# Three stages of a hybrid decoder step: samples' block scores by sample, first decay totals inside the gate projection, prompt scores from rounded halves

## The reference, cut to what matters

```python
# NSA, prompt and samples: compressed blocks, the 16 selected blocks, a window of 512
s_c = einsum('btgrd,bngd->bgrtn', q, kc) * scale - slopes * dist_c
p_c = masked_softmax(s_c, dist_c >= 0)
_, idx = top_k(score_of(p_c), 16)                      # blocks of 64 rows
ss = einsum('grd,gkld->grkl', q, k[idx]) * scale - slopes * dist    # selected
ss = einsum('bqgrd,bkgd->bgrqk', q, k_win) * scale - slopes * dist  # window
# both recurrences, in chunks, per head
b = cumsum(logf)
o = (q * exp(b)) @ S + tril(q k^T decayed by exp(b_t - b_s)) @ v
S = exp(b_last) * S + (k * exp(b_last - b))^T v
```

## Time and profile before

| | us |
|---|---|
| median of 3 runs | 4044.45 (4039.71 to 4048.02) |
| profiled execution, own time | 4041.04 |
| its span | 4039.4 |
| TensorE matmul busy | 3489.2 (86%) |
| VectorE, ScalarE, GpSimd busy | 1353.9, 1344.8, 1483.8 |

### The profile page before, as it was taken

The page is one execution under the profiler, slowest core; times in us unless marked ns, Lnnn a source line. Parts: engine busy times, 40 slices in busy tenths (PEclk is TensorE's granted clock), DMA queues, the critical chain, the costliest instruction groups (busy, mean ns, idle before and its releaser), DMA issues. The chain is left out here.

```text
span 4039.4 us, 64008 instructions
## 1 busy us (share of the span) xinstructions
PE 3489.2 (86%) x22287; PEld 3282.6 (81%) x22287; DVE 1353.9 (34%) x2028; ACT 1344.8 (33%) x2211; POOL 1483.8 (37%) x964
## 2 busy tenths in 40 slices
PE   5988887898088888799999998798997899999997
PEld 4966665898058777799999997788886799999997
DVE  3034442001003445443343332043345344343342
ACT  2134442000003443244344442233323244344442
POOL 2300001332403222246666664122222256666663
PEclk8978887899569999899999999899999899999998
DMA  1400001785200001134444443101111134444443
GB/s 71 129 17 0 0 0 48 258 266 164 78 11 32 32 32 58 59 99 139 137 138 149 144 151 106 48 28 39 51 38 54 58 114 133 138 140 133 143 137 124
DMA packets 158153, 372.99 MB, mean 92 GB/s; under 512 B 22410, under 2 KB 78026, under 8 KB 156316
## 3 DMA queue, kind: packets, MB, share of 16 engines
q1 hardware_dynamic: 116828, 310.96, 23.9%
q10 hardware_dynamic: 29440, 32.78, 2.5%
q0 software_dynamic: 11776, 27.80, 2.1%
HBM read 352.76 MB, written 22.89 MB: 93 GB/s over the span
## 5 line engine op out<-in xcount | busy, mean ns | idle before, releaser
L493 POOL TENSOR_TENSOR back_WL<-back_RAW,back_WH 128x1024 fp32r<-128x1024 f32 (+1 forms) x408 | 956.1, 2350 | 679.3 <-ACT back_WH L594 678.2
L532 PE MATMUL PS<-back_TH,back_WH 128*128 128x344 f32 x2112 | 676.9, 321 | 13.9 <-DVE back_TL L703 13.9
L532 PE MATMUL PS<-back_TL,back_WH 128*128 128x344 f32 x2112 | 674.7, 319 | 0.0
L532 PE MATMUL PS<-back_TH,back_WL 128*128 128x344 f32 x2112 | 674.4, 319 | 0.0
L594 ACT ACTIVATE back_WH<-back_RAW 128x1024 fp32r<-128x1024 f32 (+1 forms) x408 | 421.6, 1033 | 523.2 <-DMA back_RAW<-in_w 350.7
L532 PEld LDWEIGHTS PS<-back_TH,back_WH 128*128 128x128 f32 x2112 | 397.9, 188 | 15.6 <-issue 15.6
L532 PEld LDWEIGHTS PS<-back_TL,back_WH 128*128 128x128 f32 x2112 | 398.0, 188 | 0.0
L532 PEld LDWEIGHTS PS<-back_TH,back_WL 128*128 128x128 f32 x2112 | 397.8, 188 | 0.0
L741 DVE TENSOR_TENSOR back_HL<-back_TMP,back_HH 128x344 f32 x132 | 323.1, 2447 | 126.5 <-ACT back_HH L607 126.5
L1076 PE MATMUL PS<-layer_XH,layer_WH 128*128 128x344 f32 x960 | 325.9, 339 | 32.8 <-POOL layer_WL L1026 28.5
L532 PE MATMUL PS<-back_HH,back_WH 128*128 128x344 f32 x1056 | 338.4, 320 | 0.0
(11 more groups left out here) (365 smaller groups left out, 6079.3 us busy)
## 6 DMA issues: line engine op xcount, KB each, us to landing
back_RAW<-in_w SPq DMA_DIRECT2D x360, 512.0 KB, 3.3
layer_AR<-in_cmp SPq DMA_DIRECT2D x192, 128.0 KB, 4.3
layer_AR<-in_cmp POOLq DMA_DIRECT2D x192, 128.0 KB, 4.1
back_RAW<-in_w SPq DMA_DIRECT2D x48, 384.0 KB, 3.1
layer_AR<-in_cmp ACTq DMA_DIRECT2D x128, 128.0 KB, 4.1
layer_WR<-in_w_even SPq DMA_DIRECT2D x54, 256.0 KB, 2.8
layer_WR<-in_w_odd SPq DMA_DIRECT2D x50, 256.0 KB, 2.9
XT<-in_xT SPq DMA_DIRECT2D x4, 1032.0 KB, 7.8
```

Of the source, the lines that this page charges most:

```text
L493: pool.tensor_tensor(lo, raw, hi.bitcast(F32), ALU.subtract).then_inc(wl_ready, 1)
L532: mm = pe.matmul(m.PS[:, bank, 0:CH], wgt[:, t % RING, w], tok[:, k0 + k], start=(k0 + k + n == 0), stop=(last and n == 2 and k == kt - 1))
```

## The change

It does three things.

1. *Samples' block scores.* The fetch loops are written out over the samples, each sample has semaphores of its own, and TensorE takes a sample's eight instructions (two groups, two halves) as soon as its 30 blocks are in.
2. *First totals.* Chunk 0's totals move out of `steps` into the gate projection: for HGRN2 between its third and fourth piece (and the turning of the logarithms ahead of it, so TensorE waits for the logarithm first), for GLA between the two gate tiles. Chunk 1's totals follow directly behind the gate tile. `expo`, `queries` and `keys` of chunk 0 move with them; queries 1 goes behind the first product of step 0.
3. *Prompt scores.* q and the keys are split into fp32r halves. `m.QS` holds for a group q's high part on its own 64 partitions and q's low part on the others; `m.KHD` holds the high part of the keys on both halves of the partitions, `m.KL` the low part. A score is one fp32r matmul over 128 rows (high keys times both parts of q) and one over 64 rows (low keys times high q). ScalarE makes the high keys of kind 0 and VectorE their low part, GpSimd both for the window, all once ahead of the rounds; the low part of q is a VectorE subtraction per round and group.

```diff
@@ linear_attention, GpSimd @@
                 for pos in GATES:
                     lower(h, pos)
+                keys(h, 0)
                 if more:
                     lower(h + 1, 0)
-                for c in range(QT):
+                for c in range(1, QT):
                     keys(h, c)
@@ linear_attention, TensorE, opening @@
-                for pos in GATES:
-                    tile(h, pos)
                 pe.wait_ge(turn_read, h * 3 * VT + ONE)
-                if not gla:
+                if gla:
+                    tile(h, NEARLY)
+                    sums(h, 0)
+                    tile(h, NEARLY + 1)
+                else:
                     pe.wait_ge(lf_ready, h + 1 + ONE)
...
+                    for n in range(NLN):
+                        natural(h, n)
+                    for j in range(3):
+                        piece(h, NEARLY, j)
+                    pe.wait_ge(nat_read, h * NNAT + NLN + ONE)
+                    sums(h, 0)
+                    for j in range(3, 6):
+                        piece(h, NEARLY, j)
+                sums(h, 1)
+                evacuated(pe, h, ORDER.index(1 + VT))
+                for n in range(NLN, NNAT):
+                    natural(h, n)
...
             def steps(h, more):
-                sums(h, 0)
-                sums(h, 1)
                 for c in range(QT):
@@ ScalarE, opening @@
-                for pos in GATES:
-                    evac_then(h, pos, (h, pos + 1) if pos + 1 < NTL else (h + 1, 0) if more else None)
-                for n in range(NNAT):
...
+                if gla:
+                    evac_then(h, NEARLY, (h, NEARLY + 1))
+                    expo(h, 0)
+                    evac_then(h, NEARLY + 1, following)
+                else:
+                    for n in range(NLN):
+                        natural(n)
+                    evac(h, NEARLY, 0)
+                    expo(h, 0)
+                    evac(h, NEARLY, 1)
+                    if more:
+                        upper(*following)
+                    evac(h, NEARLY, 2)
+                for n in range(NLN, NNAT):
+                    natural(n)
@@ VectorE @@
+                evacuated(dve, h, ORDER.index(0))
+                queries(h, 0)
                 dve.wait_ge(smp_turned, h + 1 + ONE)
...
-                queries(0)
-                queries(1)
...
                     if c >= 1:
                         state(c - 1)
-                        if c + 1 < QT:
-                            queries(c + 1)
+                    if c + 1 < QT:
+                        queries(h, c + 1)
@@ attention, GpSimd (new) @@
+            for g in range(G):
+                for half in (halves[g], halves[1 - g]):
+                    pool.tensor_tensor(m.KHD[1][g][half], NT[halves[g], TKW, 0:SEQ],
+                                       m.ones[halves[g], 0:1].to_broadcast([DH, SEQ]), ALU.mult).then_inc(kx_ready, 1)
+            pool.wait_ge(kx_ready, 4 + ONE)
+            for half, high in zip(halves, m.KHD[1]):
+                pool.tensor_tensor(m.KL[1][half], NT[half, TKW, 0:SEQ], high[half].bitcast(F32), ALU.subtract)\
+                    .then_inc(kx_ready, 1)
@@ attention, TensorE, scores @@
-                        mm = pe.matmul(sbank(s)[:, a - k0:b - k0], m.QP[:, g, i * P:(i + 1) * P],
-                                       NT[:, TKS if kind == 0 else TKW, a:b], start=True, stop=True)
+                        pe.matmul(sbank(s)[:, a - k0:b - k0], m.QS[:, g, i * P:(i + 1) * P], m.KHD[kind][g][:, a:b],
+                                  start=True, stop=False)
+                        mm = pe.matmul(sbank(s)[:, a - k0:b - k0], m.QS[half, g, i * P:(i + 1) * P],
+                                       m.KL[kind][half, a:b], start=False, stop=True)
@@ attention, TensorE, compressed scores @@
-                        mm = pe.matmul(m.PS[:, 7, c0:c0 + PBLK], m.QP[:, g, i * P:(i + 1) * P], m.KCT,
-                                       start=True, stop=True)
+                        pe.matmul(m.PS[:, 7, c0:c0 + PBLK], m.QS[:, g, i * P:(i + 1) * P], m.KCH[:, g],
+                                  start=True, stop=False)
+                        mm = pe.matmul(m.PS[:, 7, c0:c0 + PBLK], m.QS[:, g, i * P:(i + 1) * P], m.KCL[:, g],
+                                       start=False, stop=True)
@@ attention, ScalarE @@
+            for g in range(G):
+                act.activation(m.KHD[0][g][halves[g]], NT[halves[g], TKS, 0:SEQ], ACT.Copy).then_inc(kh_ready, 1)
+            for g in range(G):
+                act.activation(m.KHD[0][g][halves[1 - g]], NT[halves[g], TKS, 0:SEQ], ACT.Copy).then_inc(kh_ready, 1)
@@ attention, VectorE @@
-            t.up(dve.memset(m.QP, 0.0))
...
+            dve.wait_ge(kh_ready, 4 + ONE)
+            for half, high in zip(halves, m.KHD[0]):
+                dve.tensor_tensor(m.KL[0][half], NT[half, TKS, 0:SEQ], high[half].bitcast(F32), ALU.subtract)\
+                   .then_inc(kl_ready, 1)
... in each round, per group, behind the bias tables:
+                    dve.wait_ge(q_ready, r * 2 + g + 1 + ONE)
+                    dve.tensor_tensor(m.QS[halves[1 - g], g:g + 1], NT[halves[g], ds(r, 1), 0:SEQ],
+                                      m.QS[halves[g], g:g + 1].bitcast(F32), ALU.subtract).then_inc(ql_ready, 1)
@@ sample_select @@
-            with eng.Fori(0, NB) as b:
+            for b in range(NB):
...
-                            .then_inc(pool_in if eng is nc.gpsimd else blocks_in, 16)
+                            .then_inc((pool_in if eng is nc.gpsimd else blocks_in)[b], 16)
...
-            pe.wait_ge(blocks_in, 20 * NB * 16)
-            pe.wait_ge(pool_in, 10 * NB * 16)
             pe.wait_ge(idx_ready, 2)
-            for half in range(2):
-                rows = slice(half * DH, (half + 1) * DH)
-                for n in range(NBG16):
+            for n in range(NBG16):
+                if n % G == 0:
+                    pe.wait_ge(blocks_in[n // G], 20 * 16)
+                    pe.wait_ge(pool_in[n // G], 10 * 16)
+                for half in range(2):
+                    rows = slice(half * DH, (half + 1) * DH)
                     mm = pe.matmul(m.PS[0:ROWS, 2 + half, :].rearrange("p (a b) -> p a b", b=BLK),
```

More of the change, by code:

```diff
@@ L1085, in tile, with natural @@
                     piece(h, pos, j)
+            def natural(h, n):
+                src = fT if n < NLN else vT[:, (n - NLN) // 2]
+                if n >= 2:
+                    pe.wait_ge(nat_read, h * NNAT + n - 1 + ONE)
+                if NLN <= n < 2 * NLN:
+                    pe.wait_ge(lnl_ready, h * NLN + n - NLN + 1 + ONE)
+                for c in range(4):
+                    j = n % 2 * 4 + c
+                    mm = turn(m.PS[:, 6 + n % 2, c * P:(c + 1) * P], src[:, j * P:(j + 1) * P])
+                mm.then_inc(nat_ready, 1)
             def opening(h):
@@ L1126, in sums @@
             def sums(h, c):
+                if c == 0:
+                    pe.wait_ge(lnl_ready, (h + 1) * (NLN or 1) + ONE)
                 pe.wait_ge(ex_ready, h * QT + c + ONE)
@@ L1291, in opening @@
                        .then_inc(nat_read, 1)
+                act.wait_ge(turn_read, h * 3 * VT + ONE)
+                following = (h + 1, 0) if more else None
+                if gla:
[13 more added lines that the diff above has]
+                    natural(n)
                 if gla:
@@ L1683, in attention, with _ @@
         ot_read = sem("ot_read")
-        zeroed = m.dve.n + 2
+        zeroed = m.dve.n + 1
+        halves = [slice(g * DH, (g + 1) * DH) for g in range(G)]
         block = ctx.enter_context(started(nc, sems))
+        @block.gpsimd
+        def _(pool):
+            for g in range(G):
[6 more added lines that the diff above has]
+                    .then_inc(kx_ready, 1)
         @block.tensor
@@ L1798, in _ @@
             t = m.dve
-            t.up(dve.memset(m.QP, 0.0))
             t.up(dve.memset(m.PC, 0.0))
+            for g in range(G):
+                for half in (halves[g], halves[1 - g]):
+                    dve.tensor_copy(m.KCH[half, g], m.KCT[halves[g]]).then_inc(kc_ready, 1)
+            dve.wait_ge(kc_ready, 4 + ONE)
+            for g in range(G):
+                for half in (halves[g], halves[1 - g]):
+                    dve.tensor_tensor(m.KCL[half, g], m.KCT[halves[g]], m.KCH[halves[g], g].bitcast(F32), ALU.subtract)\
+                       .then_inc(kc_ready, 1)
+            dve.wait_ge(kh_ready, 4 + ONE)
+            for half, high in zip(halves, m.KHD[0]):
+                dve.tensor_tensor(m.KL[0][half], NT[half, TKS, 0:SEQ], high[half].bitcast(F32), ALU.subtract)\
+                   .then_inc(kl_ready, 1)
             dve.wait_ge(t.sem, zeroed)
```

82 lines of the change are left out of this document (41 added, 41 removed).

## The result

The changed kernel takes 4228.98 us (median of 4 runs, 4222.30 to 4236.00) against 4045.13 of the kernel before in the same comparison (4 runs): a ratio of 1.0456, 95% interval 1.0432 to 1.048. It is slower by 184 us where 96 less were predicted. The profiled execution has a span of 4234.4 us, 195.0 more than before.

| stage | before | after | difference |
|---|---|---|---|
| to the first HGRN2 projection (attention and all samples' stages) | 1202.1 | 1408.9 | +206.8 |
| HGRN2, first projection to last level matmul | 422.8 | 424.5 | +1.7 |
| output projection and feed-forward of layer 0 | 879.1 | 887.6 | +8.5 |
| GLA, from there to its last level matmul | 611.3 | 583.9 | -27.4 |
| the rest, to the end of the span | 924.1 | 929.5 | +5.4 |

A forecast was written before the change was run, and what follows sets the result against it. It took TensorE's own work and the holes in it as the bound; terms -35 - 16 - 24 - 21 = -96 took 4041.0 to 3945, 3948 against the median, range 3895 to 4000.

The forecast's parts named there:

- A block costs 0.47 instead of 0.85: Prompt attention: a 512-key score block as two fp32r matmuls 0.237 us apart instead of two fp32 instructions of 0.43.
- part 3: Prompt scores from rounded fp32r halves: -21 us in all (-45 to +5), after added preparation.
- Rival A: Attention falls to half clock because shorter scores make steps too thin: +168 us, about 4150, slower; 6%.
- The heads of the rounds: Added preparation before the first compressed score: +15 us in round 0, +11.5 over rounds 1 to 3.
- the contention: Round 0: GpSimd's window-key work slows VectorE beside it, 0 to 14 us possible, 5.6 taken.
- The 10 us of the compressed scores: Compressed prompt scores: fp32r weight loads 0.11 instead of 0.22 us apart, 2.5 us saved a round, -10.
- Part 1: Samples' block scores run as each sample's blocks arrive, hiding seven of eight samples: -35 us (-28 to -44).
- The written-out loop: Samples' fetch loop unrolled: -2 us taken, between up to 8 saved and 5 lost.
- the last sample: Samples' block scores: the one burst behind the last block priced at half clock, 6.8 us; 3.4 at full clock.
- Part 2: First decay totals inside the gate projection: -16 us in the first layer, -24 in the second.
- the hole ahead of the gate tile: First layer's heads: TensorE must now wait for the logarithm before the gate tile, a new 3.6 us hole.
- 38 hoped for: Prompt attention: shorter score blocks save 9.5 us a round, -38 in all (-25 to -55).

The follow-up runs named there:

- E4: The changed kernel with 16 dense fp32r matmuls of 512 columns per round straight before the body's step 0, low keys still on 64 rows: 4019.43 us.
- E3: The changed kernel with the low-key matmul over all 128 rows instead of 64: 3966.33 us.
- E13: E3 with a matmul of 64 rows and 4 columns ahead of each block, overwritten by the block's own: 4016.57 us.
- E15: The changed kernel with both score matmuls on the group's own 64 rows, leaving out low query times high key: 4163.14 us.
- E5: The changed kernel without the low-key matmuls, one fp32r matmul over 128 rows per block of prompt scores: 3944.67 us.
- E16: E3 with the low keys of the second group set to zero, all matmuls still over 128 rows: 3972.14 us.
- E6: The changed kernel with both high, then both low matmuls in steps of two blocks, low keys on 64 rows: median 4156.13 us, ratio 1.0176.
- E1: The changed kernel without its prompt-score change (samples' block scores and first totals changed, prompt scores fp32 as before): 3968.54 us.
- E9: The kernel before with only the samples' block-score change: 3994.99 us.
- E10: E9 with TensorE waiting for all samples and matmuls in their old order, so only the fetch loops are written out: 4036.14 us.
- E8: E1 with the first two pieces of the gate tile moved ahead of the wait for the logarithm in the first layer's heads: 3950.02 us.
- E11: E9 with each sample's instructions ordered four on partitions 0 to 63, then four on 64 to 127: 4005.44 us, one run.

## Why the prediction was wrong, step by step

**The step that failed** is "A block costs 0.47 instead of 0.85" in part 3, with the clock that the sum took for granted. It counted columns and took 0.237 us from matmuls that all ran over 128 rows; the low-key matmul runs over 64. That costs twice.

First the changes, at any clock. A block of 512 keys is 0.41 + 0.42 = 0.83 us at full clock (E4) instead of 0.47. Without changes the saving would have been about the predicted 0.38: the first block of a step takes 0.49 + 0.43 = 0.92 in the kernel before (starts at 275.37, 275.86, 276.29) and 0.31 + 0.24 = 0.55 in E3. With them 0.1 of it is left. E13 prices them by themselves: 50 us in all. Against the same places of E3 a change costs 0.1 to 0.2 us at full clock and 0.1 to 0.3 at half, the least at the head of a step, where E3's matmuls stand further apart than their columns need as well. The Trainium skill ("TensorEngine Tiling (Array Packing)", Key Properties) says that changing the tiling mode drains TensorE. The traces agree, and by that rule two drains a block had to be priced.

Then the clock. Score matmuls on 64 rows keep it from rising out of the head of a round: with them E15 stays at half in three rounds of four with fewer changes than E13, which rises in all four without them; E3 and E5 rise, E16 says that the rows of the instruction count and not their data. E4 adds that it is the rise that fails: a body lifted beforehand stays at full clock. At half clock TensorE bounds every step (the waits of the changed kernel's bodies are gone, only those of the rounds' heads are left), and a round takes 166.3 us instead of 105.3. Of +254 us some 50 are changes at full clock, by E13; the other 200 are the clock, and the changes' greater length at it. How much the gaps add to the idle rows in keeping the clock down isn't separated: E6 and E15, each with a third of the changes gone, rise in some rounds, where the trace of the changed kernel has none.

**Rival A** had place and sign, with 6%. Its argument against itself was that the share of streaming columns falls only from three quarters to two thirds. Columns were the wrong count (E5 rises with half of them). Its price, +42 us a round, lacked the changes; it was 61. The clock below which it was to decide, "about 0.7", is 0.64 by its own formula; the bodies' 0.50 lies under both.

**The rest of part 3.** The heads of the rounds were priced well: TensorE's waits ahead of the compressed scores, E1's line and then E3's (idle time in the last number of each):

```profile
L1755 PE MATMUL PS<-keep,layer_AR 128*128 128x16 f32 x128 | 28.0, 375 | 22.8 <-ACT layer_AR L1792 22.8
```

```profile
L1786 PE MATMUL PS<-att_KCH,att_QS 128*128 128x16 f32 x64 | 23.2, 362 | 50.4 <-DVE att_QS L1908 50.4
```

50.4 - 22.8 = 27.6 us, predicted 15 + 11.5. The first compressed score is at 245.93 against 230.02, +15.9, and the contention is there: VectorE's two low-key subtractions take 3.27 each beside GpSimd's, where one of that width takes 1.22 alone, 4.1 us in all (5.6 were taken):

```profile
231.81 5.64 POOL L1734 TENSOR_TENSOR att_KL<-layer_AR,att_KHD 64x1024 fp32r<-64x1024 f32 x2
232.00 6.54 DVE L1873 TENSOR_TENSOR att_KL<-layer_AR,att_KHD 64x1024 fp32r<-64x1024 f32 x2
240.94 1.22 DVE L1908 TENSOR_TENSOR att_QS<-layer_AR,att_QS 64x1024 fp32r<-64x1024 f32 x1
```

The 10 us of the compressed scores didn't come: they are 32 instructions with a weight load each in both kernels, and at half clock these come 0.22 us apart in fp32r as in fp32. The 0.11 that the prediction read in the earlier trace rows was a single pair behind 512-column matmuls, which had hidden the weight loads (these start 0.43 apart, at 1366.15 and 1366.58). Now:

```profile
412.23 0.38 PE L1786 MATMUL PS<-att_KCH,att_QS 128*128 128x16 f32 x1 [8.22 <-DVE att_QS L1908]
412.46 0.36 PE L1788 MATMUL PS<-att_KCL,att_QS 128*128 128x16 f32 x1
412.68 0.36 PE L1786 MATMUL PS<-att_KCH,att_QS 128*128 128x16 f32 x1
```

With all rows (E3) rounds are 101.2 us apart instead of 105.3, with 3.9 of added preparation in them: 8.0 saved a round on scores, predicted 9.5. Four of these less 27.6 are 4 us, what is left of part 3 at its best of the 21 predicted; the trace has -6 (the last score at 634.0, before 640.0) and the runs 2 to 3.

**Part 1**: predicted -35, measured -50 (E9). The mechanism was right, two sizes were off. The written-out loop gives 9 (E10), not 2: SP's fetches take 76.5 us. And the last sample takes 3.7 us instead of 6.8, because the two row groups run side by side. These two make 10 of the 15 us; the other 5 are no more than what these runs tell from nothing. The Trainium skill ("TensorE: Matmul & The Clock Gate", Part 3) has matmuls on distinct row groups run at the same time. The prediction weighed that rule with 3.4 us beside it and left it out of the sum; the trace agrees with it.

**Part 2**: predicted -40, measured -26 (E1 less E9). Second layer: the levels start 5.0 us behind the gate tiles (2860.0 to 2865.0) instead of 10.4, and the stage is 27 shorter, predicted 24. First layer: the hole ahead of the gate tile is 3.9 us (predicted 3.6), heads come 102.1 apart in E1 instead of 105.8, the stage is 9 shorter instead of 16, since the last head, where no projection fills the steps, gives 3 back. That makes 36 us of stages in the traces against 26 by the medians; 6 of the difference is a longer stretch from HGRN2 to GLA in E1's trace, which nothing explains. In the changed kernel and in E3 even this is missing: the same waits, but heads of 105.8 us at a clock of 0.92 beside heads of 102.3 at 0.97:

```profile
1207.70:1310.00 102.30, 87.76 (x579) 83.24 (x579) 48.22 (x65) 48.83 (x87) 30.10 (x16) 0.97 0.10 32
1310.20:1416.00 105.80, 91.64 (x579) 87.07 (x579) 48.32 (x65) 49.05 (x87) 30.08 (x16) 0.92 0.09 30
```

What picks one or the other stays open. E8 says that the hole, taken on as the price of the earlier totals, needn't have been: two pieces of the tile fill it. The misses of parts 1 and 2 cancel (+15 and -14); that their sum came out is luck.

## What to carry to other kernels

Count a matmul's rows as well as its columns: fewer than 128 save nothing in a stream of full ones, and every change between the two costs 0.1 to 0.2 us at full clock; a low part that could stay on 64 rows is cheaper over all 128, where the surplus product is negligible. A kernel whose busiest stage climbs to full clock anew in every round should be judged by that climb: a change that makes it thinner can lose it altogether (here 254 us for 38 hoped for), and TensorE at 100% busy is then a sign of the loss, not of good use. Where work is independent and small, spread it over row groups, one burst for each arrival: that was the largest gain here.

## What the runs showed of the hardware

- With one of two fp32r score matmuls issued over 64 rows the clock stood at 1.2 GHz through all four rounds, from 224 to 905 us, with TensorE busy 93% of the stretch from 300 to 905 us; over 128 rows, with zeros in half of the low keys' rows, the same columns run at 2.4 GHz (E16).
- A change between 128 and 64 rows costs 0.13 us on the path at full clock (E13: 384 changes, 50 us).
- Full clock is kept where it isn't gained: E4's bodies are at 1.00 in all four rounds (270 to 345 us and the same stretches of the later ones), on the instruction stream that holds the changed kernel's at 0.50.
- Matmuls of one row group, issued behind four of the other, start beside them (E11): eight 512-column instructions in 3.7 us at half clock, 0.85 apart within a group.
- A fetch loop written out saves 0.16 us of 1.12 for each issue on SP's queue.
